# Attention on one core: rounded copies and low parts of the exponentials for two units at once, values four slots behind scores

## The reference

```python
sc = jnp.einsum('bqgrd,bngd->bqgrn', qb, kc).astype(jnp.float32) * scale
pc = jax.nn.softmax(jnp.where(cval[None, :, None, None, :], sc, NEG), axis=-1)
o_c = jnp.einsum('bqgrn,bngd->bqgrd', pc.astype(vc.dtype), vc)
...
ps = jax.nn.softmax(jnp.where(smask, ss_, NEG), axis=-1)
o_s = jnp.einsum('bqgrk,bqgkd->bqgrd', ps.astype(vsel.dtype), vsel)
...
pw = jax.nn.softmax(jnp.where(wmask[None, :, None, None, :], sw, NEG), axis=-1)
o_w = jnp.einsum('bqgrk,bkgd->bqgrd', pw.astype(vwb.dtype), vwb)
...
o = gt[..., 0:1] * unblock(o_c) + gt[..., 1:2] * unblock(o_s) + gt[..., 2:3] * unblock(o_w)
```

## Time and profile before

| | |
|---|---|
| median of 3 runs | 1920.77 us (1919.46 to 1920.78) |
| span of the profiled execution | 1917.9 us |
| TensorE busy | 1889.7 us, 99% |
| VectorE busy | 1274.0 us, 66% |
| ScalarE busy | 877.3 us, 46% |
| GpSimd busy | 508.1 us, 26% |
| attention slots | about 170 to 460 us of the span |

### The profile page before, as it was taken

One profiled execution on the slowest core, in us unless ns is written; L12 is line 12 of the kernel. 1 busy time (PEld: TensorE's weight loads), 2 busy tenths in 40 slices (PEclk: granted clock), 3 DMA queues, 4 the chain that ended last, 5 costly groups with the idle time before them and its releaser, 6 DMA issues. The chain is left out here.

```text
span 1917.9 us, 25010 instructions
## 1 busy us (share of the span) xinstructions
PE 1889.7 (99%) x8999; PEld 1542.0 (80%) x8999; DVE 1274.0 (66%) x2129; ACT 877.3 (46%) x1560; POOL 508.1 (26%) x404
## 2 busy tenths in 40 slices
PE   7999999999999999999999999999999999999999
PEld 6997666667888888888888887887888888888887
DVE  6867788987633664343347778869656666668974
ACT  4545789885433333333412414454434443444442
POOL 2002234322122332222100200004544443415620
PEclk9999999999999999999999999999999999999999
DMA  6300000011333334444265246131333333366342
GB/s 175 65 1 1 1 1 1 1 45 32 105 110 121 90 102 140 139 136 143 91 222 187 75 167 219 67 94 59 114 108 100 115 100 99 105 222 234 108 141 86
DMA packets 198503, 197.62 MB, mean 103 GB/s; under 512 B 26907, under 2 KB 153069, under 8 KB 198381
## 3 DMA queue, kind: packets, MB, share of 16 engines
q1 hardware_dynamic: 196813, 195.63, 32.5%
q10 hardware_dynamic: 1568, 0.39, 0.1%
HBM read 144.35 MB, written 51.64 MB: 102 GB/s over the span
## 5 line engine op out<-in xcount | busy, mean ns | idle before, releaser
L2168 DVE TENSOR_TENSOR pair_l<-raw,pair_h 128x512 fp32r<-128x512 f32 x80 | 69.5, 870 | 133.9 <-ACT pair_h L1497 133.9
L2986 PE MATMUL bank<-d_h,pair_h 128*128 128x512 f32 x384 | 149.4, 389 | 0.0
L2987 PE MATMUL bank<-d_l,pair_h 128*128 128x512 f32 x384 | 149.4, 389 | 0.0
L2988 PE MATMUL bank<-d_h,pair_l 128*128 128x512 f32 x384 | 149.4, 389 | 0.0
L2986 PE MATMUL bank<-actT_h,pair_h 128*128 128x512 f32 x352 | 137.2, 390 | 0.0
L2987 PE MATMUL bank<-actT_l,pair_h 128*128 128x512 f32 x352 | 137.0, 389 | 0.0
L2988 PE MATMUL bank<-actT_h,pair_l 128*128 128x512 f32 x352 | 137.0, 389 | 0.0
L2986 PE MATMUL bank<-actT_h,block_h 128*128 128x512 f32 x336 | 131.2, 390 | 0.3 <-DVE block_l L2168 0.3
L2988 PE MATMUL bank<-actT_h,block_l 128*128 128x512 f32 x336 | 130.8, 389 | 0.0
L2987 PE MATMUL bank<-actT_l,block_h 128*128 128x512 f32 x336 | 130.7, 389 | 0.0
L1293 POOL TENSOR_TENSOR side<-raw,side 128x512 f32<-128x512 f32 x44 | 57.2, 1299 | 271.7 <-DVE pair_l L2168 176.3
(11 more groups left out here) (445 smaller groups left out, 5180.3 us busy)
## 6 DMA issues: line engine op xcount, KB each, us to landing
raw<-in_w_in SPq DMA_DIRECT2D x60, 512.0 KB, 5.0
raw<-in_w_up SPq DMA_DIRECT2D x44, 512.0 KB, 5.1
gates_kept<-kept SPq DMA_DIRECT2D x40, 512.0 KB, 2.7
left_raw<-spilled SPq DMA_DIRECT2D x77, 256.0 KB, 2.7
sig_all<-gates_kept SPq DMA_DIRECT2D x24, 512.0 KB, 4.1
spilled<-spill_s SPq DMA_DIRECT2D x44, 256.0 KB, 2.0
raw<-in_w_branch SPq DMA_DIRECT2D x16, 512.0 KB, 5.4
block<-in_w_down SPq DMA_DIRECT2D x6, 1024.0 KB, 7.7
```

What stands on the lines that cost most here:

```text
L2168: nc.vector.tensor_tensor(operand_l(n), pair_source(n), operand_h(n).bitcast(F32), ALU.subtract).then_inc(pair_low, 1)
L2986: nc.tensor.matmul(out, wh, b[0][:, kt, :], start=start and kt == 0, stop=False, skip_group_check=seeded)
L2987: nc.tensor.matmul(out, wh, b[1][:, kt, :], start=False, stop=False, skip_group_check=seeded)
L2988: ins = nc.tensor.matmul(out, wl, b[0][:, kt, :], start=False, stop=stop and kt == 3, skip_group_check=seeded)
```

## The change

`LAG` becomes 4: values, evacuations, turns and finals come one slot later behind the scores (one slot more in all). For even units ScalarE makes the exponential only; for odd units it makes the exponential and then one rounded copy of both units of the pair (128x1024), once the exponential of the odd one is done and the value product four units back is done. VectorE makes one low part of the same two units, in the place where the low part of the odd unit stood. `pth_done` and `ptl_done` count pairs, and the waits on them count in pairs: the exponential of u waits for the pair that holds u - 4, the values of u for the pair that holds u. The buffers keep their size of four units, two pairs.

```diff
--- before.py
+++ after.py
@@ -218,7 +218,7 @@
 
 
 
-LAG = 3
+LAG = 4
 LEAD = 12
 RING = 4
 
@@ -1543,11 +1543,13 @@
                     at = unit_at[u]
                     act.wait_ge(s_done, at + 1)
 
-                    after(act, ptl_done, 0, u - RING + 1)
+                    after(act, ptl_done, 0, (u - RING) // 2 + 1)
                     nc.scalar.activation(pT[:, u % RING, :], bank[:, 3 + at % 2, :], ACT.Exp).then_inc(exp_done, 1)
-                    act.wait_ge(exp_done, at + 1)
-                    after(act, pv_done, 0, u - RING + 1)
-                    nc.scalar.activation(pT_h[:, u % RING, :], pT[:, u % RING, :], ACT.Copy).then_inc(pth_done, 1)
+                    if u % 2:
+                        act.wait_ge(exp_done, at + 1)
+                        after(act, pv_done, 0, u - RING + 1)
+                        both = slice((u - 1) % RING, u % RING + 1)
+                        nc.scalar.activation(pT_h[:, both, :], pT[:, both, :], ACT.Copy).then_inc(pth_done, 1)
                 if slot["heads"] is not None:
                     row_heads(slot["heads"])
                 if slot["row"] is not None:
@@ -2159,9 +2161,12 @@
             heads_squares(LAST)
 
             def low_part(u, n, j):
-                dve.wait_ge(pth_done, u + 1)
-                nc.vector.tensor_tensor(pT_l[:, u % RING, :], pT[:, u % RING, :],
-                                        pT_h[:, u % RING, :].bitcast(F32), ALU.subtract).then_inc(ptl_done, 1)
+                if u % 2 == 0:
+                    return
+                dve.wait_ge(pth_done, u // 2 + 1)
+                both = slice((u - 1) % RING, u % RING + 1)
+                nc.vector.tensor_tensor(pT_l[:, both, :], pT[:, both, :], pT_h[:, both, :].bitcast(F32),
+                                        ALU.subtract).then_inc(ptl_done, 1)
 
             def pair_low_part(n):
                 dve.wait_ge(pair_high, n + 1)
@@ -2967,7 +2972,7 @@
             def values(u, n, j):
 
                 i, kind, k0, keys, blocks, g = tasks[n]
-                pe.wait_ge(ptl_done, u + 1)
+                pe.wait_ge(ptl_done, u // 2 + 1)
                 if j == 0:
                     after(pe, evac_done, 0, n - 1)
                 if kind == "cmp":
```

## The result

The kernel after takes 1926.26 us (median of 6 runs, 1925.01 to 1927.44), the kernel before 1920.12 us (6 runs, 1919.46 to 1920.78): a ratio of 1.0026, with a 95% interval of 1.0016 to 1.0035. It is slower, by 5.0 us by the ratio and by 6.1 us between the medians; no change was forecast, with 1920.5 us, and the time lies outside the range. The profiled execution took 1925.7 us with a span of 1923.7 (before: 1917.9).

What follows compares the result with a forecast made beforehand. TensorE, busy 1889.7 of 1917.9 us, was taken as the bound. Terms 0 - 0.8 + 0.6 - 0.6 + 0.5 = -0.3 us gave a span of 1917.6, plus 2.9 for start and end: 1920.5 us, range 1916.8 to 1924.2.

Steps and rivals of the forecast that it cites:

- Instructions, base 0: Attention stage: 74 copies and 74 low parts go, but nothing is taken off TensorE, so 0.
- VectorE's lateness, -0.8: TensorE's waits for VectorE's maxima and gated outputs shrink as VectorE's work falls 4.4 us: -0.8 us, bounds 0 to -7.0.
- The structural ones gain little: Waits for gated outputs, where two adjacent turns share one bank, gain little when moved by a slot.
- Start of the stage, +0.6: First slots: TensorE restarts near 175.97, then early value products wait for double low parts: +0.6 us together.
- The forecast's last sentence: A changed pace of TensorE's matmuls (0.23 us) would make all of the forecast wrong.
- Compressed keys, -0.6: ScalarE's copy of unit 6 moves behind the compressed keys, shortening TensorE's wait and absorbing the start's loss: -0.6 us.
- Tail, +0.5: Stage end: value product 144 waits for the low part of both units: +0.5 us, bounds 0 to 0.7.
- New waits, 0: Double copy waiting for a value product, and even units' exponentials waiting for a later low part: both 0.
- The wait of the copy for a value product: ScalarE's double copy waits for the value product four units back: 0.1 or 0.2 us at most.
- Span and time: Whole program: median 2.9 us above the profiled span, taken as unchanged start and end: 1917.6 + 2.9 = 1920.5.
- the second (1925.5): Rival: value products wait for double low parts up to 0.97 us later at nine odd units: +4.8 us, chance 0.11.
- The first rival: VectorE's relief counts in full, waits for maxima and gates vanish: -6.5 us at most, 1916 as a time; chance 0.14.

Runs made afterwards that it cites:

- e5c_warm: The changed kernel with six extra TensorE matmuls in slot 3 and the wait for the last projected heads back there: 1923.50 us, 1.0015 to before.
- e8_warm_late: The changed kernel with the six extra matmuls, heads wait moved back, and VectorE's `outg_l` one slot later: 1919.97 us, 0.9995 to before.
- e12_low_warm_late: The kernel before with lag 4, double low parts, single copies, six extra matmuls and `outg_l` one slot later: 1918.94 us, 0.9989.
- e9_lag4_warm_late: The kernel before with lag 4, six extra matmuls and `outg_l` one slot later, nothing paired: 1917.34 us, 0.9984.
- e1c_lag4: The kernel before with `LAG` = 4 alone, copies and low parts single: 1922.52 us, 1.0008.
- e6_late: The changed kernel with `outg_l` one slot later, without the six extra matmuls: 1922.81 us, 1.0005 to before.
- e11_two_copies: The changed kernel with ScalarE's double copy replaced by two single copies in a row at the same place: 1929.08 us, 1.0037 to before.
- e2c_lowpair: The changed kernel with single copies again, keeping lag 4 and double low parts: 1923.30 us, 1.0013 to before.
- e10_copy_last: The changed kernel with the double copy as the last of ScalarE's work in odd slots: 1924.76 us, 1.0021 to before.
- e7_before_late: The kernel before (lag 3, nothing paired) with VectorE's `outg_l` one slot later: 1917.31 us, 0.9980.
- e3c_copypair: The changed kernel with single low parts, two in a row in the double one's place, keeping lag 4 and double copies: 1929.81 us, 1.0044 to before.

## Why the prediction was wrong

The ratios form one table:

| kernel | `outg_l` in its slot | one slot later |
|---|---|---|
| before (lag 3, nothing paired) | 1.0000 | 0.9980 |
| lag 4, six matmuls | 0.9992 | 0.9984 |
| lag 4, double low parts, six matmuls | not run | 0.9989 |
| lag 4, both double, six matmuls | 1.0015 | 0.9995 |
| lag 4, both double (the change) | 1.0026 | 1.0005 |

Read as they stand, the ratios say that lag 4 gives 0.0008 back. But the clock also falls in many executions of the kernel before. The mean granted clock of its 87 executions beside the experiments was 1.000 in 15 (median 1919.83 us), 0.999 in 52 (1920.67) and 0.998 or 0.997 in 20 (1923.4 for the 18 at 0.998). All six of the change were at 0.998. Of the kernels with lag 4, 45 of 60 executions were at 0.998 or less without the six matmuls, and 2 of 55 with them. Every trace with a mean of 0.998 or less has a fall in the first slots. So here are the same kernels at the same mean clock, 1.000 (medians in us, number of executions; the last line, which has no such executions, at 0.998):

| kernel | `outg_l` in its slot | one slot later |
|---|---|---|
| before | 1919.83 (15) | 1916.86 (5) |
| lag 4, six matmuls | 1919.71 (8) | 1917.26 (10) |
| lag 4, double low parts, six matmuls | not run | 1919.00 (10) |
| lag 4, both double, six matmuls | 1923.16 (5) | 1919.71 (6) |
| lag 4, both double | 1926.26 (6) | 1922.84 (10) |

By this the change stands 6.43 us over before: -0.12 for the lag, 3.45 for the pairings and 3.10 for the fallen clock. Of the pairings' 3.45 us, 2.45 stand where `outg_l` is out of the way (1.74 low parts, 0.71 copies), and 1.00 goes through it: moving `outg_l` is worth 3.45 us with pairs, 2.45 without, and 2.97 in before. The traces agree, between units 8 and 144: the lag alone -0.1, double low parts 1.3 with `outg_l` in either place, double copies on top of them 2.7, or 1.4 where `outg_l` is late. The groups were run at different times, and before alone differs between them by up to 0.9 us, so single steps under 1 us are no more than likely. Shown are the move of `outg_l` (0.0020 on two kernels), the loss by the fallen clock (three pairs of kernels), the low parts' 1.3 us (two pairs of traces) and the sum.

*Instructions, base 0.* Held: TensorE's work is the same, and neither the 15.1 us off ScalarE nor what left VectorE bought any time.

*VectorE's lateness, -0.8.* Wrong sign by the stage's end. Units 8 to 32 did gain (-1.95 us, -1.29 of which the lag gives alone, and -0.6 the double low parts), which is more than the -0.8. But the waits for maxima grew afterwards: to 5.1 us, or 3.6 with the clock kept up (e5c_warm), from 2.2. "The structural ones gain little" was wrong too: the waits for gated outputs fell to 1.6 us here, to 0.6 by the lag alone and to 0.9 by moving `outg_l` alone.

*Start of the stage, +0.6.* The waits were worked out rightly: piece at 175.99 for 175.97, double low part done at 175.76 + 1.32 = 177.08 for 177.15, and in e5c_warm TensorE waits 0.27 + 0.16 = 0.43 us for it, for 0.4. **This is the first step that failed**: it took the matmuls' pace in the first slots as given, looked at which wait ends last and never at what TensorE still does in slots 0 to 3, which lose the value product that slot 3 had. The forecast's last sentence named a changed pace of the matmuls as what would void it, and gave it no price and no chance. It came for 6.8 us, cost 2.2 us up to unit 8, and is worth 2.5 to 3.1 us by the times. At lag 3 the fall comes too, in some executions; the lag makes it more frequent and longer.

*Compressed keys, -0.6.* The mechanism held, with 0.4 of the 0.7 us of their wait: it is 0.3 us in every kernel with double copies and 0.7 or 0.8 in every one with single copies. With the clock up (e5c_warm) start and keys come to -0.45 from unit 0 to 8, beside 0 in the sum.

*Tail, +0.5.* The size was right, +0.66 from unit 144 to 800 us, but by luck: the three kernels of lag 4 with single copies and low parts lose 0.53 to 0.55 there too. At unit 144:

```profile
456.27 1.23 DVE L2168 TENSOR_TENSOR pT_l<-pT,pT_h 128x1024 fp32r<-128x1024 f32 x1 [0.67 <-ACT pT_h L1552]
457.55 0.13 PEld L2984 LDWEIGHTS bank<-pT_h,v_h 128*65 128x65 f32 x1
```

The weight load stands right behind the end of the double low part, as worked out, but against single ones this costs 0.1 to 0.2 us, not 0.5. The rest belongs to the lag, 0.5 us of it between the third and the fourth product of 12 matmuls; why was not looked into.

*New waits, 0.* **This is the second step that failed.** It named what is queued behind the double copy, "the next exponential and the evacuation of outputs, which TensorE needs a slot or two later, covered by the 39.6 us of idle time". It left out `outg_h`, which is not needed by TensorE soon but by VectorE at once, in an order in which the maxima stand behind it. It followed what is delayed to TensorE only. It also looked at the double low part only for the value products that read it, and not for the maxima and gates queued behind it on VectorE. Put at nothing, all this cost some 3.4 us: 1.0 through `outg_h`, 1.7 by the double low parts and 0.7 by the double copies otherwise. The idle sum of an engine (39.6 us) says nothing of whether it is idle in the slot with the final.

The wait of the copy for a value product was read rightly, 0.1 or 0.2 us each. After the change, with the clock kept up, and for lag 4 alone:

```profile
ACT pT_h L1552 <- PE bank L2986: 7.5, 47, 0.2
```

```profile
ACT pT_h L1550 <- PE bank L2981: 12.1, 70, 0.7
```

The sum of 7.8 us in the changed kernel is not what costs: lag 4 alone has more of it, and is as fast as before at the same clock.

*Span and time.* The prediction took 2.9 us between span and median as start and end. In every execution on record the time is about 2.0 us above the span; the other 0.9 is that the profiled execution of before, with a clock of 1.000, was one of its faster ones. The forecast of 1920.5 does not depend on it, since the change was added to the median.

*The rivals.* The time came out near the second (1925.5), but not by its mechanism: the value products' waits are 1.1 us, with 4 waits for 74 pairs. Its warning, that the double part is late where VectorE idles for the double copy in more than some 15 slots, was met (21), and still cost little there; the price was paid in the maxima and gates. The first rival, that relief of VectorE counts, holds for units 8 to 32 only.

**What stays open.** With both repairs the pairings still cost 0.0011, about 2 us. In the traces, between units 8 and 144, TensorE's matmul starts are more than 0.6 us apart 6 times with both pairings (5.73 us together, e8_warm_late), 6 times with double low parts alone (5.48 us, e12_low_warm_late) and 4 times with none (3.69 us, e9_lag4_warm_late). So most of it comes with the double low parts; an order of work that would remove these waits was not tried. Why the clock falls in one execution and not in the next, and whether it is the six matmuls or the moved wait for the heads that holds it up, is open as well.

## What to carry to other kernels

When an engine works through a fixed order, an instruction that waits for a small result holds up all that is queued behind it: follow each delayed result not only to the bound engine but to every engine that waits for it in order, and put a step that nobody needs soon one slot behind its input (here 0.2% for one moved instruction). Doing two units' work in every second slot saves time on an engine that isn't the bound and delays the first of the two and all that shares the slot. Where a pipeline is made deeper, count what the bound engine still does while it fills. And before small ratios are read as causes, compare the granted clock of the executions on both sides: here the clock moved the kernel before by 3.6 us, more than most of the steps that were to be measured.

## What the runs showed of the hardware

The granted clock of TensorE fell to its lower level in the middle of a program in which it is 98% busy. Ahead of the fall in the changed kernel TensorE had waited 1.06 and 0.79 us, up to 172.73 and 174.27; before has 1.06 and 0.90 us at the same places, and no fall. In the traces without the six matmuls the stretch at the lower level is 6.8 us long in the change, e1c_lag4, e6_late and e11_two_copies, 3.4 us in e2c_lowpair, e10_copy_last and e7_before_late (lag 3), and not there in e3c_copypair and before; with the matmuls it is in none of five. Before and e7_before_late do the same up to that point, so it also differs from one execution of the same work to the next. The Trainium skill (TensorE: Matmul & The Clock Gate, section on a second HAM failure mode) tells of a kernel in which frequent short idle times between groups of matmuls make the clock go back and forth between its two levels. The trace agrees only in that short idle times went ahead of the fall; here it is one fall, where the slots begin, and not one in each loop.

Matmuls start 0.42 us apart at the lower level and 0.23 at the upper one. The stretch of 6.8 us cost 2.2 us up to unit 8, less than the 3.4 us by which half the pace would delay an engine that never waits (an estimate, half of 6.8).

Two VectorE low parts of 128x512 in a row start 0.61 us apart in the median (e3c_copypair), each 0.69 us long, and behind a double one of 1.22 us the next instruction starts 1.14 us later (after), so the pair in one saves under 0.1 us, as the prediction had it from one place. The means are longer, 778 to 828 ns for single and 1309 for double ones; what lengthens them in some slots was not looked into.
